# End of the output projection ordered by token tile, experts ranked in fewer steps, and other numbers of idle products

## The chip, the cores and the metric

The kernel runs on one core of a Trainium2 chip, in float32 throughout. The metric is the device time of one execution in microseconds. It is given as the median of several runs. A profiled execution gives the trace, and its span runs from the first to the last instruction.

The engines of the core are TensorE (PE in the profile; its weight loads are PEld), VectorE (DVE), ScalarE (ACT), GpSimd (POOL) and SyncE (SP), which here only issues transfers.

## The reference

A decoder trunk of two layers on 256 tokens of width 1024. Each layer runs four token mixers on the columns of one input projection, projects their concatenation back, adds it to the residual stream, normalises, and then runs a feed-forward block: dense in layer 0, two of eight experts for each token in layer 1.

```python
for l in range(DEPTH):                       # DEPTH = 2
    h = rmsnorm(x, attn_norm[l])
    ...                                      # four mixers: oa, ob, oc, od, 256 columns each
    mix = jnp.concatenate([oa, ob, oc, od], axis=-1).astype(x.dtype)
    x = x + mix @ w_out[l]
    h = rmsnorm(x, ffn_norm[l])
    if l % 2 == 0:
        x = x + swiglu(h, ffn_w1[l // 2], ffn_w3[l // 2], ffn_w2[l // 2])
    else:
        x = x + moe_swiglu(h, router[l // 2], moe_w1[l // 2], moe_w3[l // 2], moe_w2[l // 2])
return rmsnorm(x, final_norm)
...
logits = (h @ router)                        # moe_swiglu, 8 experts
top_vals, top_idx = lax.top_k(logits, 2)     # of equal logits the one with the lower index comes first
gates = jax.nn.softmax(top_vals, axis=-1)
```

## The kernel before

All order is written by hand: each engine has one program, and semaphores join them. The 256 tokens are two tiles of 128 (t = 0 and 1). `x_sb` holds the residual stream and `tok` the rows of the norm, both with tokens on partitions; `hT` holds features on partitions, 8 chunks of 128. PSUM has eight banks, and each use of one has a name: a producer `fills` it, a consumer `frees` it.

**The output projection.** `w_out_products(l, k2, parts)` (L1196) multiplies rows 256 k2 to 256 k2 + 255 of the weights, for each i in parts. Part i is token tile i // 2 and half i % 2 of the 1024 columns, and it adds up in bank O0 to O3. A part is two products of 512 columns. Four row blocks in the order 1, 2, 0, 3 make the sum; the last block, 3, is the recurrent mixer's, which is ready last. `recurrence` (L1212) ends with the products of block 0 for parts 0 to 2, then the transposes of the last mixer (`mix_to_features(3)`), block 0 for part 3, and block 3 for parts 0, 1, 2, 3.

**From there to the feed-forward block.** VectorE runs `add_and_norm` (L2036): it adds O0 and O1 into `x_sb`, and asks for the row scale of tile 0, which needs the squares of both halves from ScalarE (`square_sums`, L1546) and a power on GpSimd (L1808). It adds O2, scales the rows of tile 0 into `tok` (L2017, two halves), adds O3, takes the features of tile 0 out of bank F0 (`features_out`), scales tile 1, and takes out F2. TensorE transposes those rows in `rows_to_features` (L714, L724): F0 and F1 for tile 0, F2 and F3 for tile 1, eight transposes a tile. ScalarE takes F1 and F3 out (`feature_evacuation`, L1558, L1562), both after all four squares. Between the two tiles TensorE runs `first_of_block`: in layer 0 the first quarter products of the dense block (`up_first`, a product by quarters: `up_first` and `up_second` need tile 0 alone, `up_third` and `up_rest` need tile 1); in layer 1 the router's products of the first half of tile 0.

**The router's stage in layer 1.** `experts` (L1348) runs the other router products into bank RT. On VectorE `gates` (L2503) finds the best and the second expert, each by two maxima, a product with a descending table and two comparisons, writes the choice in four copies (`chosen_ready`), and computes the gates. TensorE counts places with triangular products into bank POS; VectorE turns them into places and the one-hot `pick` (`picks`); TensorE gathers the rows of the first expert by products with `pick` into G0 and G1; ScalarE and VectorE take these out to `slot_h`; a small product into IX gives the rows of the slots; and the loop over experts begins (`pe.Fori`, one turn an expert). While TensorE waits it runs idle products: `between_blocks(n)` (L703) has n blocks, each with the same number of columns: of the first `HALVED` blocks two products of 64 columns (4 instructions), of the rest one of 128 (2 instructions). At the start `WARM_UP` products of 256 columns and `WARM_UP_SHORT` of 64 columns do the same.

**Queues.** SP issues the weights in an order written out: for layer 1 the rows of expert 0 go into the slots of the ring that the projections leave, among them slot 3 after the last use of row block 0 of `w_out` (`w_out_used`) and slot 4 after O3 is full. Inside the loop each weight row of the next expert is asked for when its place is free.

Of the kernel before, what the change touches and what calls it, by code (L numbers as in the profile page):

```python
# [83 lines left out]
for _name, _n in (("ident", 128), ("inv_freq", 32), ("rev_cum", 128), ("rev_all", 128), ("c_mask", 128), ("a_mask", 256),  # L84
# [3 lines left out]
                  ("iota", CAP), ("token", NT), ("spare", 1)):  # L88
# [22 lines left out]
def shape_constants():  # L111
# [30 lines left out]
    put("spare", SEQ + np.arange(P)[:, None])  # L142
    put("inv_freq", (np.float32(ROPE_THETA) ** (-np.arange(0, HD, 2, dtype=np.float32) / np.float32(HD)))[None, :])
# [115 lines left out]
def build(nc, t_in, out):  # L259
    ctx = ExitStack()  # L260
    with ctx:
# [166 lines left out]
        r_tmp, r_oh = small[:, 128:144], small[:, 144:160]  # L428
        r_s = sb("r_s", [P, 8])
        passes_i = sb("passes_i", [P, 1], I32)  # L430
        descend = sb("descend", [P, N_EXPERTS])
# [249 lines left out]
        def _(pe):  # L681
# [32 lines left out]
            def rows_to_features(names, l, which, sums=None, first=None):  # L714

                if sums is not None:
                    wait_evacuated(pe, *sums)
                for t in range(NT):
                    for i in range(2):
                        name = names[2 * t + i]  # L720
                        pe.wait_ge(sem("h_ready"), 2 * (NT * norm_index(l, which) + t) + i + 1)
                        wait_open(pe, name, l)
                        for c in range(4):
                            last = nc.tensor.transpose(bank(name, l)[:, c * P:(c + 1) * P],  # L724
                                                       tok[:, t, (4 * i + c) * P:(4 * i + c + 1) * P], ident)
                        fills(last, name, l)
                    if t == 0 and first is not None:
                        first()
# [98 lines left out]
            def layer_mixers(l):  # L827
# [11 lines left out]
                rows_to_features(names, l, 0, ("dn0", l - 1) if l else None, first_of_layer)  # L839
# [374 lines left out]
            def recurrence(l):  # L1214
# [288 lines left out]
            for l in range(DEPTH):  # L1503
# [294 lines left out]
        def _(pool):  # L1798
# [86 lines left out]
            for i in range(N_EXPERTS):  # L1885
                g.memset(descend[:, i:i + 1], float(N_EXPERTS - i))
# [814 lines left out]
```

## Time and profile before

| | us |
|---|---|
| median of 3 runs | 948.43 (947.99 to 950.49) |
| profiled execution, time | 948.73 |
| profiled execution, span | 946.9 |
| TensorE busy in the span | 926.2 (98%) |
| VectorE, GpSimd, ScalarE busy | 425.0, 215.6, 181.2 |
| mean granted TensorE clock | 0.994 of full |

The time of the profiled execution is 1.83 us more than its span. In the trace a busy share says how much an engine did; what sets the time is the chain of work that ended last, which the page gives by engine and line, and the trace in order of time. A float32 product here is two matmul instructions, and a row with x32 is 32 of those. L683 is the line of the helper that records nearly all matmuls, and L1988 that of nearly all VectorE tensor operations, so that rows are told apart by their tiles and times.

### The profile page before, as it was taken

What the parts mean: (1) busy time and instruction counts of PE and PEld (TensorE: products, weight loads), DVE (VectorE), ACT (ScalarE), POOL (GpSimd) and SP (SyncE); (2) the same over time, 40 slices, a digit from 0 to 9 for tenths busy, and PEclk for the clock granted to TensorE, in tenths of its full rate; (3) what the DMA queues carried; (4) which work ended last, traced back from release to release, by engine and by line L of the source; (5) the groups of instructions that cost most, each with busy time, mean ns of one, the idle gap of its engine ahead of it and who ended that gap; (6) DMA issues with size and microseconds to landing.
All of it is one profiled execution on the core that took longest, in us unless ns stands there. A gap on an engine that the chain in (4) does not pass through costs nothing.

```text
span 946.9 us, 30492 instructions
## 1 busy us (share of the span) xinstructions
PE 926.2 (98%) x13688; PEld 741.7 (78%) x13688; DVE 425.0 (45%) x871; ACT 181.2 (19%) x416; POOL 215.6 (23%) x213
## 2 busy tenths in 40 slices
PE   8999999999999999999999999999999999999996
PEld 7897875699999644799787569686969696969692
DVE  4854666587666545795376442212121303030204
ACT  3354141211111000314525020000000101010102
POOL 3820632133333433572072100010101000000000
PEclk9999999999999999999999989999999999999999
DMA  9843201555555545454310898999999999999931
GB/s 318 278 151 118 91 2 46 170 167 169 169 168 169 210 172 172 139 172 137 103 51 2 299 374 315 339 381 400 398 400 387 413 386 414 385 411 388 396 128 44
DMA packets 90122, 223.30 MB, mean 236 GB/s; under 512 B 6080, under 2 KB 53952, under 8 KB 89920
## 3 DMA queue, kind: packets, MB, share of 16 engines
q1 hardware_dynamic: 86528, 212.29, 60.8%
q0 software_dynamic: 1680, 5.90, 2.6%
q10 hardware_dynamic: 1840, 4.00, 1.3%
q8 instruction: 61, 1.00, 0.4%
q14 instruction: 13, 0.11, 0.0%
HBM read 215.89 MB, written 6.29 MB: 235 GB/s over the span
## 4 chain that ended last, share of the span: by engine, by line
PE 94%; DVE 2%; ACT 2%; issue 1%; DMA 0%; POOL 0%; DVEq 0%; POOLq 0%; ACTq 0%
PE bank L683 92%; DVE x_sb L1988 1%; PE bank L1412 1%; DVE tok L2017 0%; PE bank L694 0%; ACT arena L1719 0%; DVE hT L1988 0%; DMA x_sb<-in_x 0%; ACT tok L1554 0%; PE bank L724 0%; PE bank L1138 0%; ACT arena L1716 0%; DVE tok L1988 0%; ACT arena L1568 0%; POOL small L1808 0%
## 5 line engine op out<-in xcount | busy, mean ns | idle before, releaser
L683 PE MATMUL bank<-arena 128*64 128x96 f32 (+6 forms) x8592 | 504.1, 276 | 4.6 <-issue 2.3
L683 PEld LDWEIGHTS bank<-arena 128*64 128x64 f32 (+4 forms) x8592 | 380.1, 136 | 126.7 <-issue 104.6
L1988 DVE TENSOR_TENSOR arena<-arena 128x512 f32<-128x512 f32 (+3 forms) x139 | 129.8, 948 | 33.5 <-PE bank L683 22.4
L683 PE MATMUL bank<-arena,hT 128*128 128x256 f32 (+4 forms) x588 | 126.7, 386 | 0.2
L683 PE MATMUL bank<-hT,arena 128*64 128x128 f32 (+2 forms) x1596 | 116.2, 285 | 2.6 <-DVE hT L1988 2.6
L1988 DVE TENSOR_TENSOR arena<-arena,bank 128x128 f32<-128x128 f32 (+3 forms) x159 | 57.4, 386 | 132.3 <-ACT arena L1782 105.6
L683 PEld LDWEIGHTS bank<-hT,arena 128*64 128x64 f32 (+2 forms) x1596 | 104.4, 141 | 11.4 <-issue 5.0
L683 PEld LDWEIGHTS bank<-arena,hT 128*128 128x128 f32 (+2 forms) x588 | 81.8, 173 | 35.1 <-issue 26.8
L683 PE MATMUL bank<-tok,arena 128*64 128x128 f32 x1824 | 104.9, 273 | 0.0
L683 PEld LDWEIGHTS bank<-tok,arena 128*64 128x64 f32 x1824 | 100.7, 137 | 0.0
L1967 POOL DMA_INDIRECT x_rows<-arena,rows_out x7 | 10.1, 1447 | 210.2 <-DVE arena L2627 210.2
L1808 POOL TENSOR_TENSOR small<-small 128x1 f32<-128x1 f32 (+2 forms) x20 | 19.4, 972 | 153.6 <-DVE small L2008 80.8
L1568 ACT COPY arena<-bank 128x512 f32<-128x512 f32 (+2 forms) x51 | 24.1, 476 | 127.8 <-PE bank L683 125.6
L1778 ACT ACTIVATE arena<-bank 128x480 f32<-128x480 f32 x16 | 9.1, 570 | 198.3 <-PE bank L683 198.3
L2600 DVE COPY rows_out<-rows_next 96x1 int32<-96x1 int32 x8 | 1.2, 150 | 98.1 <-PE bank L683 98.1
L1852 POOL TENSOR_TENSOR arena<-arena 128x1024 f32<-128x1024 f32 x11 | 27.1, 2468 | 51.4 <-PE bank L683 44.3
L1959 POOL DMA_INDIRECT tok<-h_rows,rows_in x8 | 7.7, 959 | 122.8 <-DVE gate_next L2585 122.8
L2625 DVE COPY arena<-bank 64x512 f32<-64x512 f32 x8 | 5.5, 694 | 55.2 <-PE bank L683 55.2
L2615 DVE COPY arena<-bank 32x256 f32<-32x256 f32 x32 | 13.5, 421 | 34.4 <-PE bank L683 34.0
L1854 POOL TENSOR_TENSOR arena<-arena 128x512 f32<-128x512 f32 x10 | 16.8, 1678 | 43.6 <-PE bank L683 43.6
L1988 DVE TENSOR_TENSOR arena<-bank,consts 128x512 f32<-128x512 f32 x26 | 17.2, 688 | 19.2 <-PE bank L683 18.6
L1750 ACT ACTIVATE arena<-arena 128x256 f32<-128x256 f32 x22 | 9.2, 417 | 70.4 <-DVE arena L1988 70.4
(224 smaller groups left out, 673.1 us busy)
## 6 DMA issues: line engine op xcount, KB each, us to landing
arena<-in_moe_w SPq DMA_DIRECT2D x128, 704.0 KB, 11.8
arena<-in_moe_w SPq DMA_DIRECT2D x40, 1024.0 KB, 9.5
arena<-in_ffn_w SPq DMA_DIRECT2D x33, 1024.0 KB, 5.5
arena<-in_w_in SPq DMA_DIRECT2D x22, 1024.0 KB, 6.2
arena<-in_w_out SPq DMA_DIRECT2D x8, 1024.0 KB, 4.9
arena<-in_moe_w SPq DMA_DIRECT2D x8, 512.0 KB, 13.2
arena<-in_w_in SPq DMA_DIRECT2D x2, 1088.0 KB, 5.5
consts<-in_consts SPq DMA_DIRECT2D x1, 1330.5 KB, 6.2
```

Of the source, the lines that this page charges most:

```text
L683: return nc.tensor.matmul(o, lhsT, rhs, start=start, stop=stop, skip_group_check=True)
L1412: last = nc.tensor.transpose(banks[b][:, c * CAP:(c + 1) * CAP], slot_rows[:, (c0 + c) * P:(c0 + c + 1) * P], ident[0:CAP, 0:CAP])
L1568: frees(nc.scalar.copy(dst, src), name, l)
L1750: nc.scalar.activation(silu_tmp[:, j % 2, :], corners[j % 2][:, 0:SEQ], ACT.Silu).then_inc(sem("silu"), 1)
L1778: nc.scalar.activation(slot_silu[:, 5 * b:5 * b + 5, :], banks[b][:, 0:5 * CAP].rearrange("p (c s) -> p c s", c=5), ACT.Silu).then_inc(fre ...
L1808: g.tensor_tensor(ap_out, ap_in, m_half[:, 0:n], ALU.pow).then_inc(sem("rstd_ready"), 1)
L1852: last = g.tensor_tensor(weight_sums(n)[:, 2], w11, w21, ALU.subtract)
L1854: last = g.tensor_tensor(weight_sums(n)[:, 2], w22, w12, ALU.subtract)
L1959: g.indirect_dma_start(slot_rows, None, h_rows, bass.IndirectOffsetOnAxis(rows_in[:, 0:1], 0)).then_inc(sem("gathered"), 16)
L1967: g.indirect_dma_start(x_rows, bass.IndirectOffsetOnAxis(rows_out[:, 0:1], 0), slot_y, None, compute_op=ALU.add).then_inc(sem("scattered") ...
L1988: return v.tensor_tensor(o, a, b, op)
L2615: last = v.tensor_copy(slot_y[HALF:CAP, c * GW:(c + 1) * GW], banks[6 - c // 2][c * QUARTER:(c + 1) * QUARTER, 0:GW])
```

## The change

It has five parts.

1. `w_out`: the mixer's transposes come ahead of block 0's part 2; then follow block 3's parts 0 and 1, block 0's part 3, block 3's part 2, **the transposes of tile 0**, and block 3's part 3. On VectorE the features of tile 0 (F0) come ahead of the addition of O3; on ScalarE those of F1 come ahead of the square of O3's half.
2. Between the two tiles TensorE now runs `up_first` twice and one `up_second` in layer 0, and both halves of the router's products of tile 0 in layer 1.
3. `gates` ranks each expert: it counts how many logits are greater, or equal with a lower index, in 8 by 8 comparisons, and takes rank below 2. `chosen_ready` comes with the first copy, the others follow; the gates are normalised by a sum. One of four writes of `place` stands ahead of `pick`. The table `descend` and its 8 memsets go, and a constant table of 64 columns comes.
4. The slots of G1 are taken out by one operation in place of four.
5. Idle products: 6, 2, 2 blocks in place of 14, 6, 4, the first 10 halved in place of 12; at the start 3 wide and 37 short in place of 4 and 20.

```diff
-                w_out_products(l, 0, (0, 1, 2))
+                w_out_products(l, 0, (0, 1))
                 pe.wait_ge(sem("mix_ready"), NT * (l + 1))
                 mix_to_features(3, l)
+                w_out_products(l, 0, (2,))
+                w_out_products(l, 3, (0, 1))
                 w_out_products(l, 0, (3,))
-                w_out_products(l, 3, (0, 1, 2, 3))
+                w_out_products(l, 3, (2,))
+                tile_to_features(("F0", "F1", "F2", "F3"), l, 1, 0)
+                w_out_products(l, 3, (3,))
...
             def dense(l):
-                wait_evacuated(pe, "F1", l)
-                for j in range(2):
-                    up_second(l, 0, j)
+                up_second(l, 0, 1)
...
             def experts(l):
-                router_products(l, 0, 1)
                 for i in range(2):
                     router_products(l, 1, i)
-                between_blocks(14)
+                between_blocks(6)
...
-                between_blocks(6)
+                between_blocks(2)
...
-                between_blocks(4)
+                between_blocks(2)
...
                         for j in range(2):
                             up_first(l, 0, j)
+                        wait_evacuated(pe, "F1", l)
+                        up_second(l, 0, 0)
                     else:
-                        router_products(l, 0, 0)
-
-                rows_to_features(names, l, 1, ("O0", l), first_of_block)
+                        for i in range(2):
+                            router_products(l, 0, i)
+
+                first_of_block()
+                tile_to_features(names, l, 1, 1)
...
-            def square_sums(k):
+            def square_sums(k, names=None, l=None):
                 for t in range(NT):
...
                     for i in range(2):
+                        if t and i and names:
+                            tile_evacuation(names, l, "ffn_norm", 0)
...
                 asked = ask_row_scale(k, 0)
                 add_bank(prefix, l, 2)
                 scale_rows(asked, 0)
+                dve.wait_ge(sem("gains_landed"), 16 * (m + 1))
+                if prefix == "O":
+                    features_out(names[0], m, gain, 0)
                 add_bank(prefix, l, 3)
                 half_mean(k, 1)
-                dve.wait_ge(sem("gains_landed"), 16 * (m + 1))
-                features_out(names[0], m, gain, 0)
+                if prefix != "O":
+                    features_out(names[0], m, gain, 0)
...
-                first_of(lg3, best, oh)
-                link(stt(tm, oh, -3.0e38, lg3, ALU.mult, ALU.add))
-                first_of(tm, second, cb)
-                link(tt(oh, oh, cb, ALU.add))
+                shape = [P, NT, N_EXPERTS, N_EXPERTS]
+                other, own = lg3.unsqueeze(2).broadcast_to(shape), lg3.unsqueeze(3).broadcast_to(shape)
+                tt(above, other, own, ALU.is_gt)
+                link(tt(equal, other, own, ALU.is_equal))
+                earlier = const("earlier").rearrange("p (e f) -> p e f", e=N_EXPERTS)
+                link(tt(equal, equal, earlier.unsqueeze(1).broadcast_to(shape), ALU.mult))
+                link(tt(above, above, equal, ALU.add))
+                link(v.tensor_reduce(rank, above, AX_X, ALU.add))
...
-                for e8 in tables:
-                    last = v.tensor_copy(chosen[:, :, e8], oh)
-                last.then_inc(sem("chosen_ready"), 1)
+                oh = chosen[:, :, tables[0]]
+                v.tensor_scalar(oh, rank, 2.0, None, ALU.is_lt).then_inc(sem("chosen_ready"), 1)
...
-                for q in range(MAX_PASSES + 1):
+                link(v.tensor_scalar(place[:, :, tables[0]], at, 0.0, None, ALU.add))
+                one_hot(pick, 0, chosen).then_inc(sem("picks"), 1)
+                for q in range(1, MAX_PASSES + 1):
                     v.tensor_scalar(place[:, :, tables[q]], at, -float(CAP * q), None, ALU.add)
...
                     wait_full(dve, "G1", l)
-                    for c in range(4, 8):
-                        last = slots_in(c, 0)
-                    frees(last, "G1", l)
+                    at = PARAM["ffn_norm"][0] + KC // 2
+                    frees(tt(slot_h[:, KC // 2:, :], bank("G1", l)[:, 0:4 * CAP].rearrange("p (c s) -> p c s", c=4),
+                             along(params[:, at:at + KC // 2], CAP), ALU.mult), "G1", l)
...
-WARM_UP = 4
-WARM_UP_SHORT = 20
-HALVED = 12
+WARM_UP = 3
+WARM_UP_SHORT = 37
+HALVED = 10
```

## Rows read from the trace of the kernel before

**Rows 1.** The page: TensorE's busy time, and the chain that ended last, by engine.
```profile
PE 926.2 (98%) x13688; PEld 741.7 (78%) x13688; DVE 425.0 (45%) x871; ACT 181.2 (19%) x416; POOL 215.6 (23%) x213
...
PE 94%; DVE 2%; ACT 2%; issue 1%; DMA 0%; POOL 0%; DVEq 0%; POOLq 0%; ACTq 0%
```

**Rows 2.** Timeline, layer 1, output projection to router: start, duration, engine, line, operation.
```profile
550.41 0.69 DVE L1988 TENSOR_TENSOR x_sb<-x_sb,bank 128x512 f32<-128x512 f32 x1 [1.03 <-PE bank L683]
...
552.15 0.68 DVE L1988 TENSOR_TENSOR x_sb<-x_sb,bank 128x512 f32<-128x512 f32 x1
552.31 0.55 POOL L1808 TENSOR_TENSOR small<-small 128x1 f32<-128x1 f32 x1 [12.52 <-DVE small L2008]
...
552.99 0.88 DVE L2017 TENSOR_SCALAR tok<-x_sb,small 128x512 f32<-128x512 f32 x2 [0.16 <-POOL small L1808]
...
553.64 1.04 PE L724 MATMUL bank<-consts,tok 128*128 128x128 f32 x8
553.84 0.69 DVE L1988 TENSOR_TENSOR x_sb<-x_sb,bank 128x512 f32<-128x512 f32 x1
...
555.62 0.64 PE L683 MATMUL bank<-router_sb,hT 128*64 128x8 f32 x16 [0.94 <-DVE hT L1988]
...
556.35 0.88 DVE L2017 TENSOR_SCALAR tok<-x_sb,small 128x512 f32<-128x512 f32 x2 [0.67 <-POOL small L1808]
...
556.89 1.82 PE L724 MATMUL bank<-consts,tok 128*128 128x128 f32 x8 [0.64 <-DVE tok L2017]
...
558.75 1.14 ACT L1562 ACTIVATE hT<-bank,params 128x128 f32<-128x128 f32 x4 [2.38 <-PE bank L724]
```

**Rows 3.** Timeline, layer 0: tile 0, first quarters, tile 1, then second quarters and on.
```profile
178.72 1.04 PE L724 MATMUL bank<-consts,tok 128*128 128x128 f32 x8
...
180.70 1.97 PE L683 MATMUL bank<-hT,arena 128*64 128x128 f32 x32 [0.94 <-DVE hT L1988]
...
182.59 1.09 PE L724 MATMUL bank<-consts,tok 128*128 128x128 f32 x8
...
183.62 3.71 PE L683 MATMUL bank<-hT,arena 128*64 128x128 f32 x64
183.72 1.14 ACT L1562 ACTIVATE hT<-bank,params 128x128 f32<-128x128 f32 x4 [2.28 <-PE bank L724]
```

**Rows 4.** Windows, layer 1: stretch, its length, busy us (x instructions) by engine; PEclk is granted clock.
```profile
557.00:563.95 6.95, 6.95 (x82) 6.62 (x83) 3.10 (x15) 1.14 (x4) 0.00 (x0) 0.51 1.02 413
563.95:568.27 4.32, 4.32 (x51) 4.13 (x49) 1.86 (x15) 0.31 (x2) 0.00 (x0) 1.00 0.44 175
```

**Rows 5.** Timeline, layer 1, from the router's result to the loop.
```profile
561.23 4.64 PE L683 MATMUL bank<-consts 128*64 128x64 f32 x52
561.43 0.17 DVE L2511 COPY small<-bank 128x16 f32<-128x16 f32 x1 [2.84 <-PE bank L683]
...
564.09 0.41 DVE L2529 COPY arena<-small 128x16 f32<-128x16 f32 x4
...
565.80 1.28 PE L683 MATMUL bank<-arena,consts 128*128 128x8 f32 x10
...
567.65 0.57 DVE L2499 TENSOR_SCALAR arena<-consts,arena 128x96 f32<-128x96 f32 x2
...
568.28 2.90 PE L683 MATMUL bank<-arena,tok 128*64 128x96 f32 x64
...
571.01 1.04 PE L683 MATMUL bank<-consts 128*64 128x128 f32 x8
571.31 0.99 DVE L2574 TENSOR_SCALAR arena<-bank,params 128x96 f32<-128x96 f32 x4 [0.99 <-PE bank L683]
```

**Rows 6.** Groups of VectorE by form: count, busy us, mean ns of one, idle before.
```profile
L1988 DVE TENSOR_TENSOR arena<-arena,bank 128x128 f32<-128x128 f32 x78 | 20.2, 283 | 13.8 <-ACT arena L1746 13.4
L1988 DVE TENSOR_TENSOR arena<-arena,bank 128x480 f32<-128x480 f32 x16 | 10.5, 655 | 2.6 <-PE bank L683 2.6
```

**Rows 7.** Timeline, first turn of the loop: two gaps of TensorE that nothing in the trace releases.
```profile
594.17 5.50 PE L683 MATMUL bank<-arena 128*64 128x96 f32 x128 [0.80 <-issue]
...
601.19 8.76 PE L683 MATMUL bank<-arena 128*64 128x96 f32 x177 [1.53 <-issue]
```

**Rows 8.** The chain in order of time, one full turn: start, us, what.
```profile
655.67 44.10 PE bank L683 x840
```

**Rows 9.** Timeline, start of the kernel.
```profile
1.09 5.76 PE L683 MATMUL bank<-hT 128*64 128x256 f32 x48 [1.09 <-POOL hT L1882]
...
7.67 1.06 PE L724 MATMUL bank<-consts,tok 128*128 128x128 f32 x8 [0.82 <-DVE tok L2017]
...
10.57 1.14 ACT L1562 ACTIVATE hT<-bank,params 128x128 f32<-128x128 f32 x4 [0.59 <-PE bank L724]
...
11.12 5.20 PE L683 MATMUL bank<-hT,arena 128*128 128x256 f32 x23 [0.59 <-DVE hT L1988]
```

More of the change, by code:

```diff
@@ L87 @@
                   ("reset64", 256), ("reset128", 512), ("all", 128),
-                  ("iota", CAP), ("token", NT), ("spare", 1)):
+                  ("iota", CAP), ("token", NT), ("spare", 1), ("earlier", N_EXPERTS * N_EXPERTS)):
     CONST[_name] = (_at, _n)
@@ L142, in shape_constants @@
     put("spare", SEQ + np.arange(P)[:, None])
+    e = np.arange(N_EXPERTS)
+    put("earlier", np.reshape(e[None, :] < e[:, None], (1, -1)))
     put("inv_freq", (np.float32(ROPE_THETA) ** (-np.arange(0, HD, 2, dtype=np.float32) / np.float32(HD)))[None, :])
@@ L712, in between_blocks, with tile_to_features @@
                         idle_products(1, banks[2], ident[:, 0:HALF], consts[:, 0:P])
[L714 to L728, printed above, removed]
+            def tile_to_features(names, l, which, t):
+                for i in range(2):
+                    name = names[2 * t + i]
+                    pe.wait_ge(sem("h_ready"), 2 * (NT * norm_index(l, which) + t) + i + 1)
+                    wait_open(pe, name, l)
+                    for c in range(4):
+                        last = nc.tensor.transpose(bank(name, l)[:, c * P:(c + 1) * P],
+                                                   tok[:, t, (4 * i + c) * P:(4 * i + c + 1) * P], ident)
+                    fills(last, name, l)
             def wait_features(names, l, k):
@@ L1555, in square_sums, with tile_evacuation @@
                                              accum_out=ss[:, 2 * t + i:2 * t + i + 1]).then_inc(sem("squares"), 1)
[L1557 to L1564 removed]
+            def tile_evacuation(names, l, gain, t):
+                name = names[2 * t + 1]
+                wait_full(act, name, l)
+                for c in range(4):
+                    last = nc.scalar.activation(hT[:, 4 + c, t * P:(t + 1) * P], bank(name, l)[:, c * P:(c + 1) * P],
+                                                ACT.Copy, scale=param(gain, 4 + c))
+                frees(last, name, l)
             def evacuate(name, l, dst, src):
@@ L1581, in layer_mixers @@
             def layer_mixers(l):
-                feature_evacuation(("T0", "T1", "T2", "T3"), l, "attn_norm")
+                for t in range(NT):
+                    tile_evacuation(("T0", "T1", "T2", "T3"), l, "attn_norm", t)
                 if l == 0:
@@ L2506, in gates @@
                 lg3 = logits.rearrange("p (t e) -> p t e", t=NT)
-                oh = r_oh.rearrange("p (t e) -> p t e", t=NT)
-                tm = r_tmp.rearrange("p (t e) -> p t e", t=NT)
                 cb = comb.rearrange("p (t e) -> p t e", t=NT)
-                best, second, rank = r_s[:, 2:4], r_s[:, 4:6], r_s[:, 6:8]
+                rank = r_tmp.rearrange("p (t e) -> p t e", t=NT)
+                above, equal = [moe("y")[:, P * i:P * i + P].rearrange("p (t e f) -> p t e f", t=NT, e=N_EXPERTS)
+                                for i in range(2)]
@@ L2511, in gates @@
                 frees(v.tensor_copy(logits, bank("RT", l)[:, 0:16]), "RT", l)
                 wait_evacuated(dve, "RT", l)
-                def first_of(src, top, o):
-                    link(v.tensor_reduce(top, src, AX_X, ALU.max))
-                    for t in range(NT):
-                        last = stt(o[:, t, :], src[:, t, :], top[:, t:t + 1], descend[:, :], ALU.is_equal, ALU.mult)
-                    link(last)
-                    link(v.tensor_reduce(rank, o, AX_X, ALU.max))
-                    link(tt(o, over(descend[:, :], NT), along(rank, N_EXPERTS), ALU.is_equal))
@@ L2533, in gates @@
-                tt(r_s[:, 0:2], second, best, ALU.subtract).then_inc(sem("gates_shifted"), 1)
+                shape = [P, NT, N_EXPERTS, N_EXPERTS]
[4 more added lines that the diff above has]
+                link(tt(equal, equal, earlier.unsqueeze(1).broadcast_to(shape), ALU.mult))
```

38 lines of the change are left out of this document (17 added, 21 removed).

## The prediction, as it was put on record

> **What bounds the kernel now.** I first read the page: TensorE is busy for 98% of the span and makes 94% of the chain that ended last [rows 1]. So an edit pays only where TensorE stands still, or runs work that is no product of the model, with the chain passing through it. The chain in order of time leaves TensorE at few places, and two of these lie in the change: the handoff from the output projection to the feed-forward block (once a layer) and the router's stage ahead of the expert loop. The timelines of both follow. A full turn of the loop is TensorE back to back [rows 8] and is untouched, so it only moves as a whole: what is won or lost before it arrives at the end in full.
>
> In the handoff of layer 1, part 3 of block 3 ends at 553.64 and the transposes of tile 0 follow at once. Then TensorE stands for 0.94 us until F0's features are out, does 0.64 us of router products, and stands from 556.27 to 556.89 for tile 1 [rows 2]. In layer 0 there is the same 0.94, but then 1.97 us of first quarters carry TensorE up to tile 1's transposes, and nothing is idle after that [rows 3]. In the router's stage VectorE's ranking runs from 561.43 to 564.50, yet the products that use it begin at 565.80, as 52 idle instructions queued ahead of them last until 565.87 [rows 5].
>
> **Step 1, the handoff up to tile 0.** Ahead of tile 0's transposes stand the same products as before less one part. A part takes 552.15 - 550.41 = 1.74 us by the two additions that its end releases [rows 2], so TensorE comes to these transposes about 1.7 us earlier, at 551.95. But what they wait for doesn't move: on VectorE the scaling of tile 0 stays queued behind the addition of O2, and O2's last part is still the fifth of the same products. The row scale itself is ready earlier, since O0 and O1 end a part sooner; it then waits for O2. So scaling starts at 552.99 as before. Tile 1's transposes began 556.89 - 556.35 = 0.54 after theirs, so tile 0's start at 553.53: 1.58 us of standing still that the part had covered. With the second half of the rows (553.87) they end at about 554.6.
>
> **Step 2, from O3 to tile 1.** The last part now runs from 554.6 to 556.3, where it ended at 553.64. Its addition starts 0.2 later, at 556.5. From that addition to tile 1's transposes the chain (addition, square, scale, power, scaling) took 556.89 - 553.84 = 3.05 us [rows 2], and each link of it is unchanged; F0 and F1 are taken out during the last part and don't stand in its way. Tile 1 starts at 559.55, 2.65 us later.
>
> In layer 0 this is partly covered. After the last part TensorE has three quarter products, 2.95 us by 1.97 for two [rows 3], against a wait of 3.25. Put on that layer's clock, tile 1's transposes start at 184.6 instead of 182.59. They take 1.09, and ScalarE's F3 another 1.14 and 0.1 of handing over, so F3 is out at 186.95. One quarter product (0.98) is left to cover that, where there were two: the third quarters start at 186.95, against 183.62 + 1.97 = 185.59. **Layer 0 loses 1.35 us**; I bound it by 1.0 and 1.6. TensorE has no idle time after this point, so nothing gives it back. What is late next is the feature sums on VectorE, due only after 2 us of third quarters. The transfers behind `w_out_used` and O3 go out 3.4 and 2.7 us later; in layer 0 they bring weights for the third pair of column blocks, tens of microseconds ahead. In layer 1 they are four rows of expert 0, which must land before the loop (570), and have 14 us.
>
> **Step 3, layer 1 up to the ranking.** Router products of tile 0 (2 x 0.64) fill part of the wait and are off the path. Then tile 1 from 559.55. At full clock it takes 1.09 as in layer 0, ScalarE 1.14, the last router product 0.64, and with handing over VectorE starts at 562.7, 1.3 later than now. At half clock tile 1 takes 1.82 [rows 2] and the router product about 1.3, which gives 564.0. The trace shows half clock here: granted 0.51 (1.2 GHz) from 557.00 to 563.95 and 1.00 (2.4 GHz) behind it [rows 4]; before it fell TensorE had done transposes and narrow products with two gaps. The new stretch of that kind is longer, so I expect a fall in it too, but can't say where. I take it between tile 1 and the last router product: 563.3.
>
> **Step 4, the ranking.** Removed: a chain of 3.07 us up to the fourth copy. Added: a copy (0.17), four operations of 128 elements, one reduction of 128 and one comparison. The nearest row for 128 elements is 283 ns [rows 6]; small ones take 0.17 each [rows 5]. 0.21 + 5 x 0.29 + 0.2 = 1.9 us, as one pair overlaps. Bounds: 1.4 (0.2 for each) and 2.3. TensorE's 6 blocks are 24 instructions of 64 columns. Eight of 128 columns take 1.04 at full clock [rows 5], so 24 take 1.6; of the 52 now, the 2.7 us at half clock are about 27 instructions, 0.10 each, which makes 2.4. TensorE starts them 0.2 ahead of VectorE. So the place products start at 1.95 (full) to 2.2 (half) behind the ranking's start, against 4.37. From 562.7, 563.3 or 564.0 that is 564.65, 565.5 or 566.2, against 565.80: -1.15, **-0.3**, +0.4.
>
> **Step 5, places, gather, G1.** From place products to gather it is 568.28 - 565.80 = 2.48 now. One write of `place` in place of four and the copy of the counts goes ahead of `pick`: 1.28 + 0.05 + 0.21 + 0.57 + 0.06 = 2.2, so -0.3. The later copies and the best logit are hidden behind the 1.28 us of products; if that cover fails they cost 0.1 each. Behind the gather, TensorE's 1.04 us of idle products and VectorE's four operations (571.31 to 572.30) end together. They become half a microsecond and one operation of 384 elements, which by 0.66 for 480 [rows 6] is 0.55: **-0.4**. `passes_ready` moves behind `pick` by the three writes, 0.4, and is still ready before the gather ends. Layer 1 in sum: -0.3 - 0.3 - 0.4 = **-1.0**, with bounds -1.85 (full clock) and -0.3 (half clock from tile 1 on).
>
> **Edits at nothing.** The start: eight wide instructions become six and 40 short ones 74. The first 48 last until 6.85 [rows 9]; the new ones end near 8.2, so tile 0's transposes start 0.5 later. That hides behind ScalarE, whose second evacuation (10.57) is released by tile 1; if the cover is gone it costs 0.5. The 8 memsets are off GpSimd's path. The mixer's transposes come 1.7 us earlier, but VectorE had the mixer ready well before, and part 2 hides their evacuation as part 3 did.
>
> **A rule on the clock.** What the row shows is in step 3. The Trainium skill (TensorE: Matmul & The Clock Gate, Part 4: PE-mode transpose) says that a transpose doesn't count as TensorE activity in the way a product does. By this rule the new 1.58 us of standing still and the 1.05 of transposes behind it are one weak stretch in both layers, and layer 0 is at risk. The trace agrees as far as it goes: the clock fell in layer 1 behind transposes, and in layer 0 it stayed, with 0.94 idle and transposes but dense products after.
>
> **Sum.** 1.35 - 1.0 = +0.35 on 948.73, the time of the profiled execution (span 946.9 and 1.83 around it): 949.1. That execution is 0.3 above the median of 948.43, so the forecast for a median is 948.8.
>
> **Rivals.**
> A, slower: the clock falls in layer 0 as well, in the new gap at about 177. For: the weak stretch (idle and transposes) grows from 2.0 to 2.6 us in one piece. Against: the last part, 1.7 us of dense products, now stands inside. The price is half of the time at half clock. Of the 6.95 seen [rows 4] that is 3.5 us, with a shorter fall about 1.7. Time 950.5 to 952.3. It decides the sign at a fall longer than 5 us.
> B, slower: in layer 1 too few idle instructions are left to bring the clock back before the gather. The 27 or so instructions that ran at half clock before 563.95 become at most 24. Then the gather takes twice its 2.90 [rows 5] and the place products 1 us more: 952 to 954.
> C, faster: the clock stays up until the loop (-1.85), and the two gaps of 2.33 us in the first turn, which no engine releases [rows 7], shrink by half with other spacing: 948.4 + 1.35 - 1.85 - 1.2 = 946.7, and 945.5 if both vanish.
> D: the reorder doesn't do what it says but costs nothing either, because the transposes find their rows without a gap. Against: VectorE's order in step 1. It gives -1.0 alone: 947.4.
>
> **How the numbers follow.** Forecast 0.60; A 0.12; B 0.10; C 0.10; D 0.08. For the range, bounds of the steps (-1.2, +1.0) and the gaps of the first turn, which may move by 1 either way, give 946.6 below. Above, it takes in the short fall of A and most of the long one: 951.9. About 0.3% (2.8 us) is what a measurement of this kernel tells from no change. Faster by more than that is only the far end of C: 0.07. Slower by more is B and half of A, with a little for unseen waits: 0.18. The rest, 0.75, is within.
>
> **What would show it.** In both layers a gap of about 1.6 us ahead of tile 0's transposes; 3.05 us from O3's addition to tile 1's transposes; in layer 0 a short gap ahead of the third quarters; `chosen_ready` 1.9 us after RT, with place products close behind. Wrong would be: tile 0's scaling ahead of O2's addition, no gap there, a granted clock of 0.5 near 177, or a half clock that lasts into the gather.

## The result and the profile after

| | before | after |
|---|---|---|
| median, us | 948.72 (8 runs) | 952.67 (8 runs, 950.42 to 955.04) |
| profiled execution: time, span | 948.73, 946.9 | 950.42, 948.6 |
| ratio of the runs | | 1.0044, 95% interval 1.0032 to 1.0057 |

The change makes the kernel 0.44% slower. The median is 3.95 us longer, and the profiled execution only 1.7: it is the fastest of the eight of after. Both numbers have to be explained, and the rows explain the smaller one first.

Timeline of after, layer 0, from the end of the output projection to the dense block (start, duration, engine, line; L684, L722 and L1992 are the L683, L724 and L1988 of before). It answers to [rows 3].

```profile
168.36 8.75 PE L684 MATMUL bank<-arena,hT 128*128 128x512 f32 x20
...
175.62 0.55 POOL L1814 TENSOR_TENSOR small<-small 128x1 f32<-128x1 f32 x1 [10.81 <-DVE small L2012]
...
177.15 0.69 DVE L1992 TENSOR_TENSOR x_sb<-x_sb,bank 128x512 f32<-128x512 f32 x1 [1.61 <-PE bank L684]
...
177.99 0.88 DVE L2021 TENSOR_SCALAR tok<-x_sb,small 128x512 f32<-128x512 f32 x2 [0.16 <-DVE x_sb L1992]
...
178.53 1.09 PE L722 MATMUL bank<-consts,tok 128*128 128x128 f32 x8 [1.42 <-DVE tok L2021]
...
181.38 0.69 DVE L1992 TENSOR_TENSOR x_sb<-x_sb,bank 128x512 f32<-128x512 f32 x1 [1.39 <-PE bank L684]
...
184.41 1.10 PE L722 MATMUL bank<-consts,tok 128*128 128x128 f32 x8 [0.30 <-DVE tok L2021]
...
186.75 1.97 PE L684 MATMUL bank<-hT,arena 128*64 128x128 f32 x32 [0.21 <-ACT hT L1567]
```

TensorE reaches tile 0's transposes at 177.1 and stands for 1.42 us. The row scale is ready at 176.17 (GpSimd's row), but its use waits for VectorE to add O2 at 177.15. The last part and its addition then come late (181.38 against 178.92), tile 1's transposes 3.03 behind that addition, and the third quarters begin at 186.75 where they began at 185.59.

Timeline of after, layer 1, the same place and the router's stage. It answers to [rows 2] and [rows 5].

```profile
557.82 0.69 DVE L1992 TENSOR_TENSOR x_sb<-x_sb,bank 128x512 f32<-128x512 f32 x1 [1.39 <-PE bank L684]
...
560.85 1.72 PE L722 MATMUL bank<-consts,tok 128*128 128x128 f32 x8 [1.10 <-DVE tok L2021]
...
564.68 2.80 PE L684 MATMUL bank<-consts 128*64 128x64 f32 x24
564.88 0.17 DVE L2518 COPY small<-bank 128x16 f32<-128x16 f32 x1 [2.43 <-PE bank L684]
...
566.60 0.18 DVE L2531 TENSOR_SCALAR arena<-small 128x16 f32<-128x16 f32 x1
...
567.41 1.54 PE L684 MATMUL bank<-arena,consts 128*128 128x8 f32 x10
...
569.20 0.57 DVE L2506 TENSOR_SCALAR arena<-consts,arena 128x96 f32<-128x96 f32 x2
...
569.93 0.16 DVE L2544 COPY arena<-bank 128x8 f32<-128x8 f32 x1
...
570.19 2.86 PE L684 MATMUL bank<-arena,tok 128*64 128x96 f32 x64 [0.63 <-DVE arena L2506]
...
573.16 0.56 DVE L1992 TENSOR_TENSOR arena<-bank,params 128x384 f32<-128x384 f32 x1 [0.85 <-PE bank L684]
```

The ranking takes 1.90 us (564.88 to 566.78) where it took 3.07. The place products still start 0.63 behind it, as 24 idle instructions at half clock last 2.80. The one-hot ends at 569.77, but the gather starts at 570.19, just behind the copy of the counts.

The first turn of the loop in after, answering to [rows 7]:

```profile
596.14 5.50 PE L684 MATMUL bank<-arena 128*64 128x96 f32 x128 [1.34 <-issue]
602.89 8.76 PE L684 MATMUL bank<-arena 128*64 128x96 f32 x177 [1.25 <-issue]
```

These gaps make 2.59 us, 0.26 more. Later turns are equal, in the chain of after as in [rows 8]:

```profile
657.37 44.10 PE bank L684 x840
```

So the profiled 1.7 us are 1.45 in layer 0 (the mixers of layer 1 start at 393.60 against 392.14), nothing in layer 1 up to the loop, and 0.26 in the first turn.

**The other 2 us.** Every execution has its mean granted clock, and times follow it. What TensorE loses by half clock is about (1 - clock) x time. In 21 runs of before, made on one chip beside the experiments, the mean clock was 0.9940, a loss of 5.7 us; in the 8 runs of after here 0.9916, a loss of 8.0, with 0.994 only in the profiled one. Take the loss off the mean times and before has 943.2, after 945.0: 1.8 more by stalls, as the profile shows, and 2.3 more by clock. All kernels below are read in this way, time and loss apart. Between 1.3 and 2.7 us of the loss of each profiled execution lie at its very end, behind TensorE's last product, and cost nothing. They aren't the same in all: the mean is 2.3 in the seven profiles with 6, 2, 2 idle blocks and 1.7 in the four with 14, 6, 4. So up to 0.7 us of a difference in loss between these two kinds may be no time at all, and the rest of a kernel with the cut would then be up to 0.7 too low.

### The profile page after: what moved, and what is told of

It is laid out like the page before. It is cut to its first block, busy times and chain, and to the rows that moved or that the text cites. A ratio compares the mean times of both kernels' runs of the same rounds, so it can differ in the third digit from the quotient of the medians.

```text
span 948.6 us, 30477 instructions
## 1 busy us (share of the span) xinstructions
PE 925.5 (98%) x13688; PEld 740.5 (78%) x13688; DVE 425.3 (45%) x861; ACT 181.3 (19%) x415; POOL 216.0 (23%) x205
## 4 chain that ended last, share of the span: by engine, by line
PE 93%; DVE 2%; ACT 2%; issue 2%; DMA 0%; POOL 0%; DVEq 0%; POOLq 0%; ACTq 0%
PE bank L684 91%; PE bank L1411 1%; DVE x_sb L1992 1%; PE bank L722 0%; PE bank L695 0%; ACT arena L1725 0%; DMA x_sb<-in_x 0%; ACT tok L1559 0%; DVE tok L2021 0%; PE bank L1136 0%; POOL small L1814 0%; ACT arena L1722 0%; DVE hT L1992 0%; ACT arena L1573 0%; DVE tok L1992 0%
## 5 line engine op out<-in xcount | busy, mean ns | idle before, releaser
L684 PE MATMUL bank<-arena 128*64 128x96 f32 (+6 forms) x8592 | 504.1, 276 | 4.8 <-issue 2.6
L684 PEld LDWEIGHTS bank<-arena 128*64 128x64 f32 (+4 forms) x8592 | 380.1, 136 | 127.0 <-issue 104.8
L1992 DVE TENSOR_TENSOR arena<-arena 128x512 f32<-128x512 f32 (+3 forms) x140 | 131.3, 952 | 33.5 <-PE bank L684 22.4
L684 PE MATMUL bank<-arena,hT 128*128 128x256 f32 (+4 forms) x588 | 127.1, 386 | 0.2
L684 PE MATMUL bank<-hT,arena 128*64 128x128 f32 (+2 forms) x1596 | 116.4, 285 | 1.8 <-DVE hT L1992 1.6
L1992 DVE TENSOR_TENSOR arena<-arena,bank 128x128 f32<-128x128 f32 (+3 forms) x159 | 57.5, 386 | 131.7 <-ACT arena L1788 105.9
L684 PEld LDWEIGHTS bank<-hT,arena 128*64 128x64 f32 (+2 forms) x1596 | 104.3, 141 | 11.4 <-issue 5.6
L684 PEld LDWEIGHTS bank<-arena,hT 128*128 128x128 f32 (+2 forms) x588 | 81.7, 173 | 34.1 <-issue 25.9
L684 PE MATMUL bank<-tok,arena 128*64 128x128 f32 x1824 | 104.9, 273 | 0.0
L684 PEld LDWEIGHTS bank<-tok,arena 128*64 128x64 f32 x1824 | 100.7, 137 | 0.0
L1992 DVE TENSOR_TENSOR arena<-bank,consts 128x512 f32<-128x512 f32 x26 | 17.2, 688 | 19.2 <-PE bank L684 18.6
```

The source lines that it names most:

```text
L684: return nc.tensor.matmul(o, lhsT, rhs, start=start, stop=stop, skip_group_check=True)
L1992: return v.tensor_tensor(o, a, b, op)
```

## The experiments

Theory H: the new gap ahead of tile 0's transposes lets the clock fall there too (rival A). Theory I: too few idle products are left in the router's stage (rival B). The first four kernels tell them apart by halves of the change. "Loss" is that by clock, "rest" the mean time without it. Each ratio is against before in runs on the same chip. Before as shown stands for the first four kernels below it; beside the next four it had a median of 949.25, a loss of 5.9 and a rest of 943.1 (35 runs), beside "later blocks back", "filled, more blocks" and "POS freed first" 950.00, 5.7 and 943.6 (13 runs), and beside "fewer products at the start" and "first blocks back" 949.50, 6.3 and 943.5 (11 runs).

| kernel | median, us | ratio to before (95%) | mean clock | loss | rest |
|---|---|---|---|---|---|
| before (21 runs) | 949.22 | | 0.9940 | 5.7 | 943.2 |
| after, again (10 runs) | 952.65 | 1.0040 (1.0027 to 1.0054) | 0.9919 | 7.7 | 944.8 |
| handoff alone (5 runs) | 953.57 | 1.0050 (1.0033 to 1.0066) | 0.9934 | 6.3 | 947.1 |
| router's stage alone (12 runs) | 948.94 | 1.0006 (0.9994 to 1.0018) | 0.9913 | 8.3 | 940.8 |
| after, old idle products (5 runs) | 953.04 | 1.0044 (1.0027 to 1.0061) | 0.9940 | 5.7 | 947.1 |
| old handoff, new ranking, old idle products (12 runs) | 949.51 | 1.0005 (0.9995 to 1.0016) | 0.9941 | 5.6 | 943.5 |
| before, idle products cut (12 runs) | 949.33 | 1.0007 (0.9996 to 1.0017) | 0.9916 | 8.0 | 941.5 |
| after, rows scaled first (12 runs) | 949.62 | 1.0009 (0.9999 to 1.0020) | 0.9911 | 8.5 | 941.2 |
| old handoff, filled (12 runs) | 947.43 | 0.9981 (0.9970 to 0.9992) | 0.9960 | 3.8 | 943.5 |
| after, later blocks back (8 runs) | 952.99 | 1.0039 (1.0024 to 1.0053) | 0.9929 | 6.8 | 946.4 |
| after, POS freed first (1 run) | 950.12 | | 0.994 | 5.7 | 944.4 |
| filled, more blocks (6 runs) | 998.99 | 1.0551 (1.0515 to 1.0586) | 0.9860 | 14.0 | 986.8 |
| the same, fewer products at the start (6 runs) | 946.54 | 0.9965 (0.9952 to 0.9979) | 0.9980 | 1.9 | 944.4 |
| after, first blocks back (6 runs) | 953.83 | 1.0054 (1.0036 to 1.0072) | 0.9928 | 6.8 | 947.8 |

### After, once more

No edit.

> The changed kernel itself once more. Its profiled execution took 950.42 us and its median is 952.67, so most executions hold some 2 us that the profiled one doesn't show. Theory H (the clock falls also in the gap ahead of tile 0's transposes): a typical execution shows a granted clock of 0.5 near 178 us or near 390 us, one more stretch of 3 to 7 us. Theory I (too few idle products are left): the only low stretch ahead of the end lies behind 555 us, and in slower executions it is longer, into the gather or the loop (past 570). Both expect 952 to 953.5 as the median, 3 to 5 above before.

Measured: 952.65. Its profiled execution took 952.06, so it shows what a typical one holds. Windows of it, layer 1 (stretch, its length, busy us and instructions of each engine, granted clock, DMA share, GB/s), and then the same of the first profiled execution of after; both answer to [rows 4].

```profile
562.60:573.00 10.40, 9.86 (x101) 9.55 (x102) 5.37 (x35) 1.35 (x5) 0.00 (x0) 0.51 0.71 288
```

```profile
561.20:567.95 6.75, 6.48 (x66) 5.93 (x64) 2.90 (x13) 1.36 (x5) 0.00 (x0) 0.50 1.02 410
```

The low stretch lasts 10.4 us and reaches into the gather, where the other ended ahead of it. In its timeline the place products take 2.30 and the gather 3.79 us:

```profile
567.45 2.30 PE L684 MATMUL bank<-arena,consts 128*128 128x8 f32 x10
569.68 1.12 PE L684 MATMUL bank<-consts 128*64 128x64 f32 x8
570.99 3.79 PE L684 MATMUL bank<-arena,tok 128*64 128x96 f32 x64 [0.19 <-issue]
```

There is no low stretch near 178 or 390, as H wanted. Theory I holds for this execution.

### The two halves alone

Handoff alone is after with the functions of before for the ranking, the evacuation of G1 and the idle products. Router's stage alone is after with before's order of the output projection and the handoff.

> The new order of the output projection and the handoff alone, with the old ranking, the old evacuation and the old idle products. Steps 1 and 2 alone give +1.2 in layer 0 and, with the old router stage behind it, +2.65 less what a short idle queue hides in layer 1, so +3.8 to +4.5 by stalls. Theory H adds 1 to 3 for the clock in layer 0: +5 to +7 over before. Theory I adds nothing: +4.

> The old handoff with the new ranking, evacuation and idle products. By stalls: ranking 1.2 and queue 1.4 earlier, gather held by the copy of the counts, loop -2.2 to -2.8 against before. Theory H: -2 to -3. Theory I: the clock stays low for longer in many executions, which eats it: -1 to +1.

Handoff alone costs 3.9 us of rest and 0.6 of loss. H had asked for 1 to 3 of clock at the gap, and its profiled execution shows full clock there. It does show half clock elsewhere in layer 0, at the end of the last mixer, where the two programs are the same. Ahead of the fall TensorE did products of 64 columns, with a gap of 0.56 us. The line of the gap in this kernel, and the window behind it, first of before and then of this kernel:

```profile
141.84 0.68 PE L683 MATMUL bank<-arena 64*64 64x64 f32 x8 [0.56 <-ACT arena L1572]
```

```profile
143.10:146.50 3.40, 3.40 (x62) 3.02 (x61) 1.58 (x4) 1.54 (x3) 1.64 (x1) 1.00 0.02 5
```

```profile
143.10:146.50 3.40, 3.40 (x28) 3.28 (x28) 1.58 (x4) 1.54 (x3) 1.64 (x1) 0.50 0.02 5
```

Output projection and gap then come 1.40 us later than in after. Two more profiles have such a stretch at the same products, "rows scaled first" in layer 0 and "later blocks back" in layer 1 (from 520.1), so it comes with the new and with the old numbers of idle products, and can explain part of the scatter between executions.

The router's stage alone wins 2.4 us of rest and gives back 2.6 in loss; in its profiled execution, at a clock of 0.994, it took 946.40, and most others had 0.990 to 0.992. The halves, 4.35 and -0.3 by the medians, add up to 4.1, near the 3.4 to 3.95 of the change.

### After with the old numbers of idle products

```diff
-                between_blocks(6)
+                between_blocks(14)
...
-                between_blocks(2)
+                between_blocks(6)
...
-                between_blocks(2)
+                between_blocks(4)
...
-WARM_UP = 3
-WARM_UP_SHORT = 37
-HALVED = 10
+WARM_UP = 4
+WARM_UP_SHORT = 20
+HALVED = 12
```

> The changed kernel with the old numbers of idle products, at the start too. By stalls the place products wait for the idle queue again, +1.5 to +2.5 over the changed kernel at an equal clock. Theory I: the clock comes back sooner, so that the sum is 0 to -2 against the changed kernel (951 to 953). Theory H: +2 over the changed kernel, 954 to 955.

The loss is 5.7 again, as in before, and the rest 2.3 higher: the median hardly moves. So the cut of idle products is an even trade: it frees the queue by as much as it costs in clock. The numbers at the start go back here too; see the next section.

### Ranking without the cut, and the cut without the ranking

The first is router's stage alone with the old numbers of idle products; the second is before with only these numbers changed.

> The old handoff and the old numbers of idle products (14, 6, 4, at the start 4 and 20), with the new ranking, gather and G1 evacuation. Theory I (the cut of idle products costs clock, and that eats what the shorter stage wins): the mean granted clock of the runs is that of before (0.994), and the ranking is hidden by the 52 idle instructions, so only the G1 evacuation is left: -0.2 to -0.8 against before. Rival Q (the new ranking itself, by its later copies and the gather held by bank 7, causes the clock loss): the clock is that of the kernel with the old handoff and the new idle numbers, 0.991, and the time +0.5 to +2.

> The kernel before with only the numbers of idle products changed (6, 2, 2 blocks, 10 halved, at the start 3 and 37). Theory I: mean clock 0.991, by which TensorE loses 2.5 to 3 us; won back are 1.3 us that the place products stood behind the idle queue: +0.5 to +2 against before. Rival Q: clock 0.994, time -1.0 to -1.5.

The loss follows the idle products and not the ranking: 5.6 with the old numbers, 8.0 with the new. Rival Q falls. The new ranking and the single operation for G1 win nothing behind the old queue (rest +0.3), where 0.2 to 0.8 us less than before was expected, and the cut alone wins 1.7 of rest for 2.3 of loss (1.6 and 2.1 against before on the same chip).

In these runs the numbers at the start change together with the blocks, and no kernel tells them apart. But none of the fifteen profiled executions has half clock in its first 143 us, and the filled kernel below, with 3 and 37 at the start, loses 3.8 us in all. So the start is an unlikely source, though not ruled out. Where the missing clock goes is seen in few profiles. With fourteen blocks ahead of the ranking all five have one stretch of some 7 us at half clock in the router's stage. With six blocks and no filling four of seven have the same, two have one of some 10 us, and one falls twice. That one is the second kernel here. Two windows of it:

```profile
557.10:564.30 7.20, 6.74 (x80) 6.23 (x79) 3.54 (x20) 1.14 (x4) 0.00 (x0) 0.53 1.01 408
...
567.80:571.00 3.20, 3.20 (x44) 3.20 (x42) 0.94 (x9) 1.04 (x4) 0.00 (x0) 0.50 0.36 138
```

The clock came back at 564.2. TensorE then did place products, 8 short idle instructions and stood for 0.53 and 0.58 us, and the clock fell again under the gather, which took 4.52 us:

```profile
566.84 4.52 PE L683 MATMUL bank<-arena,tok 128*64 128x96 f32 x64 [0.58 <-DVE arena L2499]
```

### After with the rows of tile 0 scaled ahead of O2

```diff
                 asked = ask_row_scale(k, 0)
+                if prefix == "O":
+                    scale_rows(asked, 0)
                 add_bank(prefix, l, 2)
-                scale_rows(asked, 0)
+                if prefix != "O":
+                    scale_rows(asked, 0)
```

> The changed kernel with VectorE scaling the rows of tile 0 ahead of adding O2. If the gap ahead of tile 0's transposes is due to that queue alone, it shrinks from 1.4 us to below 0.2, all behind it comes 1.4 earlier in both layers, and the time is 2.0 to 3.0 below the changed kernel (949.7 to 950.7). If ScalarE's or GpSimd's share of the row scale held it as well, the gap stays above 0.7 and the gain is below 1.5.

3.0 us below after, by medians on two chips. Timeline, layer 0, TensorE:

```profile
170.74 8.75 PE L684 MATMUL bank<-arena,hT 128*128 128x512 f32 x20
179.33 1.04 PE L722 MATMUL bank<-consts,tok 128*128 128x128 f32 x8
180.20 1.88 PE L684 MATMUL bank<-arena,hT 128*128 128x512 f32 x4
```

The gap of 1.42 is gone, so it was VectorE's queue alone. By rest (941.2) this is still 0.4 above the same kernel with the old handoff (940.8): even without the gap the new order wins nothing.

### Bank POS freed ahead of the one-hot

```diff
-                one_hot(pick, 0, chosen).then_inc(sem("picks"), 1)
                 for q in range(1, MAX_PASSES + 1):
                     v.tensor_scalar(place[:, :, tables[q]], at, -float(CAP * q), None, ALU.add)
                 frees(v.tensor_copy(count, bank("POS", l)[:, 16:24]), "POS", l)
+                one_hot(pick, 0, chosen).then_inc(sem("picks"), 1)
```

> The changed kernel with the copy of the counts (which frees bank POS) and the three later writes of place ahead of the one-hot, as before. In the changed kernel the gather began 0.42 us behind the end of the one-hot, with the copy that frees the bank ending just ahead of it. If the gather waits for the bank: it now begins within 0.1 of the one-hot's end, and place products to gather stay at 2.6 to 2.8 us, so the early one-hot had won nothing. If it waits for something else, 0.4 stays between them.

This kernel ran once, with the profiler. The one-hot (570.07, two of 0.56 together) ends at 570.63 and the gather begins at 570.69:

```profile
570.69 2.86 PE L684 MATMUL bank<-arena,tok 128*64 128x96 f32 x64 [0.58 <-DVE arena L2506]
```

So in after the gather waits for the bank, and place products to gather is 2.71 here against 2.78: the early one-hot had won nothing.

### Keeping the clock in the handoff

Router's stage alone, with eight idle products (the later expectation counts ten) where TensorE stands in layer 1:

```diff
                 tile_to_features(names, l, 1, 0)
+                if l % 2:
+                    wait_evacuated(pe, "O0", l)
+                    idle_products(3, banks[2], ident[:, 0:HALF], consts[:, 0:P])
                 first_of_block()
+                if l % 2:
+                    idle_products(2, banks[2], ident[:, 0:HALF], consts[:, 0:P])
                 tile_to_features(names, l, 1, 1)
...
+                idle_products(1, banks[2], ident[:, 0:HALF], consts[:, 0:P])
                 router_products(l, 1, 0)
+                idle_products(2, banks[2], ident[:, 0:HALF], consts[:, 0:P])
                 router_products(l, 1, 1)
```

> The old handoff, the new router stage and idle numbers, and 10 more idle products of 128 columns in layer 1 where TensorE stands in the handoff (3 behind tile 0's transposes, 2 behind the first router products, 1 and 2 around the second half's). If the clock falls in layer 1 for lack of activity between 553.6 and 561, it stays up in most executions: mean clock 0.995 or more, transposes of tile 1 in 1.1 us in place of 1.8, and 3 to 4 us below before (945 to 946). If transposes and narrow products count for nothing and the fillers are too thin, the clock is 0.991 to 0.993 and the time within 1 of before.

947.43: 1.8 us below before, where 3 to 4 were expected. In its profiled execution the clock stays up through the handoff, and falls in the gather instead. Windows:

```profile
553.90:565.20 11.30, 9.75 (x141) 8.64 (x142) 7.00 (x28) 3.25 (x13) 0.56 (x1) 1.00 1.02 412
565.20:568.90 3.70, 3.70 (x52) 3.70 (x54) 1.76 (x15) 1.00 (x4) 0.00 (x0) 0.54 0.59 235
```

### Filled, with more blocks, and the loop's code

On top of it, blocks 8, 4, 3 and POS freed first (the edit above):

```diff
-                between_blocks(6)
+                between_blocks(8)
...
-                between_blocks(2)
+                between_blocks(4)
...
-                between_blocks(2)
+                between_blocks(3)
...
-HALVED = 10
+HALVED = 15
```

> The old handoff with ten idle products in its gaps in layer 1, the new ranking, bank POS freed ahead of the one-hot, and idle blocks 8, 4, 3. Its predecessor with 6, 2, 2 lost the clock in the gather in its profiled execution (gather 4.5 us in place of 2.9). If the clock now stays up throughout: loss by the clock 3 us or less, 945.5 to 946.5, 3 below before. If it falls all the same: as its predecessor, 947 to 948.

998.99, 50 us slower, a plain miss. Ahead of the loop all went as meant; the loop is what changed. Pieces of its chain in order of time:

```profile
766.14 0.81 PE bank L1412 x8
766.95 9.59 PE bank L684 x44
776.54 2.62 issue
779.16 4.74 PE bank L684 x72
```

In each turn TensorE stands still for 3.4 to 6.3 us in all, in gaps of up to 2.8 that nothing in the trace releases, of the kind that only the first turn had. Some 8 of the 50 us are clock, as the table has it: its profile has seven short falls from 598 on. Its page counts the blocks of instructions loaded, and the line of before stands first:

```profile
q8 instruction: 61, 1.00, 0.4%
```

```profile
q8 instruction: 125, 2.05, 0.8%
```

The 64 more loads fall in the loop, 9 in each of the seven later turns, where before and after load none from the second turn on. The gaps go with these loads: each of the 28 gaps without a releaser in this trace from 580 to the end of the loop, and both of the first turn in before and in after, end 2.3 to 2.9 us behind the start of the latest load. The next kernel takes 18 products away at the start, where nothing waits for them:

```diff
-WARM_UP = 3
-WARM_UP_SHORT = 37
+WARM_UP = 4
+WARM_UP_SHORT = 18
```

> The kernel that took 999 us, with 18 products fewer at the start (4 wide and 18 short), so that TensorE has as many matmul instructions ahead of the loop as before and as the changed kernel (13,688 in all in place of 13,724). Theory L (the loop's code lies at another place among the blocks in which instructions are loaded, and no longer stays loaded; its 52 us are TensorE waiting for code in every turn): instruction loads fall from 125 to 61, a turn takes 44.9 us again, and the time is 945 to 946.5, as the loop starts near 568.5 in place of 572.3. Rival W (the earlier start of the loop, or the clock, makes the weight rows come too late in every turn): still 990 or more.

Loads are 61 again, a turn is 44.9, and the median is 946.54: 3 us faster than before on the same chip and some 6 faster than after on others. Theory L holds and W falls, as the loop starts as early as in the kernel that took 999 us. In this one's profile the clock stays up through the whole stage. The window from the handoff to the loop, and two pieces of its first turn:

```profile
553.90:569.00 15.10, 14.53 (x235) 13.30 (x234) 9.23 (x43) 4.28 (x17) 0.55 (x1) 1.00 0.90 360
```

```profile
590.39 5.50 PE L684 MATMUL bank<-arena 128*64 128x96 f32 x128 [0.40 <-issue]
597.41 8.76 PE L684 MATMUL bank<-arena 128*64 128x96 f32 x177 [1.52 <-issue]
```

### Which of the cut groups

After with blocks 6, 6, 4 (and the first 12 halved), and after with 14, 2, 2 (the first 10), against 6, 2, 2 and 14, 6, 4 above. Both keep 3 and 37 at the start.

> The changed kernel with the idle blocks ahead of the gather and of the loop put back (6, 6, 4 in place of 6, 2, 2), the first group left at 6. Loss by the clock is 1 - mean granted clock, times the time: 7.8 us in the changed kernel and 5.7 with all blocks back. If the later groups are what holds the clock through the gather: loss 5.5 to 6.5 and the time 1 to 2 below the changed kernel (951 to 952). If the first group is what brings it back: loss stays 7.5 to 8.5 and the time is 952.5 to 953.5.

> The changed kernel with 14 blocks in the first group of idle products and 2 and 2 in the others. Loss by the clock was 7.8 us with 6, 2, 2, 6.8 with 6, 6, 4 and 5.7 with 14, 6, 4. If the first group brings the clock back: loss 5 to 6.2, and 1.0 to 1.5 more of stalls, as the ranking is hidden again: 952.5 to 953.5. If it is the later groups alone: loss 7.5 to 8.5, and 954 to 955.

Both losses are 6.8 us, halfway between 7.7 and 5.7, and no expectation was met in full. But before itself lost 5.7 beside the first and 6.3 beside the second. With a scatter of 1.3 to 2 us from run to run and 8 and 6 runs, how much either group gives back is not shown. The rest is up by 1.6 and 3.0, more than the +2.3 of all blocks back in one case, so single tenths mean nothing here; that both cuts had won something in stalls is all that can be read from it.

## Why the prediction was wrong

The forecast was 948.8 (946.6 to 951.9), and the measured 952.67 lies above it.

**Steps 1 and 2, right.** The gap ahead of tile 0's transposes was put at 1.58 and is 1.42. The way from O3's addition to tile 1's transposes was put at 3.05 and is 3.03 in both layers. The third quarters were to start 1.35 later and start 1.16 later, and layer 0 as a whole loses 1.45. The run with the rows scaled first shows the cause named in step 1.

**Step 3, right in the time.** The ranking starts 2.0 later than before once layer 0's 1.45 is taken off; 1.9 was taken (563.3). The fall came sooner than it was taken to: at 561.2, which is 0.3 us into tile 1's transposes and not behind them, so they took 1.72 and both last router products ran at half clock.

**Step 4, its first term right, its second too small.** `chosen_ready` comes after 1.90 us, as said. The 24 idle instructions at half clock take 2.80 and not 2.4, so the place products come 2.53 behind the ranking's start in place of 2.2. The 2.4 rests on a wrong count: at 2.80 / 24 = 0.117 each, the 2.7 us at half clock in before were some 23 instructions and not 27. Place products start 0.16 later than before, layer 0's 1.45 taken off, where -0.3 was forecast.

**Step 5, wrong in one wait.** The prediction put the copy of the counts ahead of the one-hot. The diff has it behind, and the gather's first half goes into the bank that this copy frees. With the place products partly at half clock (1.54 for 1.28) the way to the gather was 2.78 in place of 2.2, which is +0.3 where -0.3 was forecast. The last term was right, -0.48 for -0.4. So of the forecast -1.0 for layer 1 nothing is left: +0.16 + 0.30 - 0.48 = -0.02.

So the stalls were forecast at +0.35 and came to +1.7, with the 0.26 of the loop's first turn. On 948.73 that gives 950.4, inside the range.

**The step that failed is the clock.** The sum kept the loss by clock of one profiled execution as if the change left it alone, and gave the other case (rival B) a chance of 0.10. The lower clock is the usual case and not a rare one: in 18 executions of after the mean loss was 7.8 us against 5.7, and the runs with the cut alone and with the cut undone tie it to the idle products. B named the cause. Its place, half clock up to the gather, is seen in one of the two profiles of after. Its price was too high: 3 to 5 us over the forecast, where the loss grew by 2.1. That the measured 952.67 lies within B's 952 to 954 is luck, as it took 1.35 us more of stalls than the sum on which B stands. B's argument, 27 instructions at half clock against at most 24, rests on the wrong count above; by 23 against 24 it would not have warned. Rival A fell: none of the eight profiled executions with the new handoff has a low stretch near 178 or 390; the two in layer 0 that exist, at 143, are in another stage. The rule of the Trainium skill on transposes (TensorE: Matmul & The Clock Gate, Part 4: PE-mode transpose) that was set beside it isn't refuted by that: the last part's dense products follow the weak stretch there. Rivals C and D didn't come.

The change as a whole: the handoff alone costs 4.4 us by the medians. In its profile the loop starts 5.1 later than in before, of which 1.4 is the fall at 143, 1.45 layer 0 and 2.3 layer 1 (some 0.8 come back behind that). The router's stage wins up to 2.4 by stalls and loses them in clock.

## What to carry to other kernels

Moving work of one engine earlier wins nothing while its input stays queued on another behind the same event: look up what each operand waits for before moving its user. Idle products are not only a delay, so judge a cut of them over many executions, with the granted clock of each beside its time; one profile hides it. And count the instructions ahead of a large loop: if an edit changes their number, check that the loop still loads no code in its later turns.

## What the runs showed of the hardware

A loop of 848 matmul instructions a turn ran with no instruction loads after its first turn at 13,688 and at 13,704 matmul instructions in the kernel, and with 9 loads in every turn at 13,724, the added ones being ahead of it; a turn then took 50 to 54 us in place of 44.9. A load is 2.05 MB / 125 = 16 KB. That the place of the loop in memory decides this was inferred from these counts and the run that took 18 products away, and the exact bound wasn't tried. The Trainium skill (Runtime: NRT & Kernel Launch, Instruction fetch mechanics) gives TensorE 128 KiB for instructions, filled in blocks of 16 KiB; the size of a load agrees. By these figures eight blocks fit, and nine loads a turn are one block more; that this is the reason is an estimate and not shown.

In one kernel the mean granted clock ranges from 0.992 to 0.997 from run to run, and the time follows it by 0.8 to 0.9 us for 0.001. So the execution that happened to be profiled was 2 us better than the typical one for the kernel after, and not for the kernel before. The same products ran at half clock in some executions and at full clock in others, at 143 in two profiles of fifteen.
